# Order of additions, roundings, squares and weight splits at the seams of the second block

## The reference

```python
a = _rmsnorm(h, g_pre_mix[l])
u = jnp.einsum("bsd,dc->bsc", a, w_in[l])
# ... convolution, attention, w_out, h = h + _rmsnorm(y, g_post_mix[l])
f_in = _rmsnorm(h, g_pre_ffn[l])
gt = jnp.einsum("bsd,df->bsf", f_in, w_gate[l])
up = jnp.einsum("bsd,df->bsf", f_in, w_up[l])
```

## Time and profile before

| | |
|---|---|
| median of 3 runs | 1757.17 us (1757.05 to 1759.24) |
| profiled execution: its time | 1758.98 us |
| profiled execution: span from first to last instruction | 1757.2 us |
| mean granted TensorE clock | 0.995 |
| TensorE busy | 1716.0 us (98%) |
| VectorE busy | 1256.5 us (72%) |
| ScalarE busy | 818.7 us (47%) |
| transfers | 158.29 MB, mean 90 GB/s |

### The profile page before, as it was taken

The page is one execution under the profiler, slowest core; times in us unless marked ns, Lnnn a source line. Parts: engine busy times, 40 slices in busy tenths (PEclk is TensorE's granted clock), DMA queues, the critical chain, the costliest instruction groups (busy, mean ns, idle before and its releaser), DMA issues.

```text
span 1757.2 us, 21518 instructions
## 1 busy us (share of the span) xinstructions
PE 1716.0 (98%) x8215; PEld 1413.4 (80%) x8215; DVE 1256.5 (72%) x1915; ACT 818.7 (47%) x1345; POOL 37.8 (2%) x87
## 2 busy tenths in 40 slices
PE   8999999999999999999999999999999999999998
PEld 7887888888888777778888888788888788888886
DVE  6666358687888667765778788889987645765766
ACT  7433244343445656764433443542767532333342
POOL 0000000000001121000000000000000000000000
PEclk9999999999999999999999999999999999999999
DMA  7222442333412211116142423033100353234212
GB/s 251 84 73 84 129 135 76 117 97 107 136 45 62 64 49 61 48 49 192 48 144 71 134 72 120 12 98 106 49 13 13 90 174 96 72 92 141 66 49 84
DMA packets 195749, 158.29 MB, mean 90 GB/s; under 512 B 5248, under 2 KB 161280, under 8 KB 195648
## 3 DMA queue, kind: packets, MB, share of 16 engines
q1 hardware_dynamic: 194240, 154.16, 29.1%
q0 software_dynamic: 400, 1.25, 0.3%
q10 hardware_dynamic: 1008, 1.53, 0.2%
HBM read 154.81 MB, written 2.10 MB: 89 GB/s over the span
## 4 chain that ended last, share of the span: by engine, by line
PE 89%; DVE 6%; ACT 3%; issue 1%; DMA 0%; POOL 0%; DVEq 0%; SPq 0%; ACTq 0%
PE ps L1061 28%; PE ps L1063 28%; PE ps L1062 28%; PE ps L1565 1%; PE ps L1131 1%; ACT sb L2021 1%; DVE sb L2238 1%; ACT sb L1764 1%; PE ps L1454 0%; DVE sb L2236 0%; DVE sb L2495 0%; DVE sb L2264 0%; PE ps L1190 0%; DVE sb L2737 0%; ACT sb L1770 0%
## 5 line engine op out<-in xcount | busy, mean ns | idle before, releaser
L1061 PE MATMUL ps<-sb,sb 128*128 128x512 f32 (+3 forms) x2435 | 927.6, 387 | 9.7 <-ACT sb L2021 5.2
L1063 PE MATMUL ps<-sb,sb 128*128 128x512 f32 (+3 forms) x2435 | 911.6, 379 | 0.0
L1062 PE MATMUL ps<-sb,sb 128*128 128x512 f32 (+3 forms) x2435 | 910.9, 379 | 0.0
L2238 DVE TENSOR_TENSOR sb<-sb,sb 128x1024 fp32r<-128x1024 f32 (+1 forms) x414 | 404.8, 997 | 219.0 <-ACT sb L1764 218.2
L1061 PEld LDWEIGHTS ps<-sb,sb 128*128 128x128 f32 (+1 forms) x2435 | 450.8, 188 | 110.2 <-issue 11.9
L1764 ACT ACTIVATE sb<-sb 128x1024 fp32r<-128x1024 f32 (+1 forms) x414 | 349.7, 871 | 394.3 <-PE ps L1063 389.1
L1063 PEld LDWEIGHTS ps<-sb,sb 128*128 128x128 f32 (+1 forms) x2435 | 450.4, 188 | 86.6
L1062 PEld LDWEIGHTS ps<-sb,sb 128*128 128x128 f32 (+1 forms) x2435 | 451.1, 188 | 81.8 <-issue 0.2
L2478 DVE TENSOR_TENSOR sb<-sb,sb 128x1024 fp32r<-128x1024 f32 x70 | 85.5, 1222 | 47.5 <-ACT sb L1926 45.2
L1921 ACT ACTIVATE sb<-sb 128x512 f32<-128x512 f32 x64 | 40.3, 631 | 130.8 <-DVE sb L2530 130.8
L2460 DVE TENSOR_TENSOR sb<-sb,sb 128x1024 f32<-128x1024 f32 x80 | 95.1, 1217 | 0.6
(11 more groups left out here) (217 smaller groups left out, 1107.2 us busy)
## 6 DMA issues: line engine op xcount, KB each, us to landing
sb<-in_w_up SPq DMA_DIRECT2D x86, 512.0 KB, 4.1
sb<-in_w_down SPq DMA_DIRECT2D x86, 512.0 KB, 4.8
sb<-in_w_gate SPq DMA_DIRECT2D x22, 512.0 KB, 3.9
sb<-in_a_w_in SPq DMA_DIRECT2D x20, 512.0 KB, 3.8
sb<-in_w_in SPq DMA_DIRECT2D x20, 512.0 KB, 3.7
sb<-in_w_o SPq DMA_DIRECT2D x16, 512.0 KB, 3.7
sb<-in_w_mem_kv SPq DMA_DIRECT2D x8, 512.0 KB, 7.5
sb<-in_w_out SPq DMA_DIRECT2D x8, 512.0 KB, 3.8
```

What stands on the lines that cost most here:

```text
L1061: mm(ps, lh, rh, start=start, stop=False, **k)
L1062: mm(ps, lh, rl, start=False, stop=False, **k)
L1063: return mm(ps, ll, rh, start=False, stop=stop, **k)
L2238: tt(lo, raw, hi, ALU.subtract).then_inc(S("w_lo"), parts)
```

## The change

Two kinds of order are changed; no instruction is added or removed.

For the second layer of the first block (l = 1) alone, the last two additions of the feed-forward, `("rd", 3, 6)`, come ahead of the split of slab g0 (the `w` step). On ScalarE and TensorE this swap changes nothing, as only VectorE has a `rd` step.

At both seams ScalarE rounds columns 4 to 7 directly behind columns 0 to 3, then splits the second tile's slab, then squares row slabs 2 and 3; before, it was squares, split, columns 4 to 7. VectorE likewise forms the remainders of columns 4 to 7 ahead of the second tile's slab.

```diff
-        plan += [("P", 3, 6), ("rd", 3, 5), ("rdu", 3, 0), ("w", PS[l, 3, 6] + 3), ("rd", 3, 6)]
+        plan += [("P", 3, 6), ("rd", 3, 5), ("rdu", 3, 0)]
+        plan += [("w", PS[l, 3, 6] + 3), ("rd", 3, 6)] if l == 0 else [("rd", 3, 6), ("w", PS[l, 3, 6] + 3)]
         return plan
...
             square(X, "pre_mix", t)
         for k in range(4):
             turn("pre_mix", Ah, "pre_mix", k)
+        for k in range(4, 8):
+            turn("pre_mix", Ah, "pre_mix", k)
+        weights(SL["in", "g0"] + 2)
         for t in range(2, 4):
             square(X, "pre_mix", t)
-        weights(SL["in", "g0"] + 2)
-        for k in range(4, 8):
-            turn("pre_mix", Ah, "pre_mix", k)
         rsqrt("pre_mix", 4)
...
             square(X, "pre_ffn", t)
         for k in range(4):
             turn("pre_ffn", Ah, "pre_ffn", k)
+        for k in range(4, 8):
+            turn("pre_ffn", Ah, "pre_ffn", k)
+        weights(SL["gt", 0] + 2)
         for t in range(2, 4):
             square(X, "pre_ffn", t)
-        weights(SL["gt", 0] + 2)
-        for k in range(4, 8):
-            turn("pre_ffn", Ah, "pre_ffn", k)
         rsqrt("pre_ffn", 4)
...
         for k in range(4):
             turn("pre_mix", Ah, Al, "pre_mix", k)
-        weights(SL["in", "g0"] + 2)
         for k in range(4, 8):
             turn("pre_mix", Ah, Al, "pre_mix", k)
+        weights(SL["in", "g0"] + 2)
         stats("pre_mix")
...
         for k in range(4):
             turn("pre_ffn", Ah, Al, "pre_ffn", k)
-        weights(SL["gt", 0] + 2)
         for k in range(4, 8):
             turn("pre_ffn", Ah, Al, "pre_ffn", k)
+        weights(SL["gt", 0] + 2)
         stats("pre_ffn")
```

## The result

The changed kernel took 1762.21 us (median of 19 runs, 1759.15 to 1763.84), the kernel before 1759.12 us in as many runs beside it (1756.76 to 1761.62): ratio 1.0018, 95% interval 1.0012 to 1.0024, so 3.2 us slower (2.1 to 4.2). The profiled execution of the changed kernel spans 1759.5 us, 2.3 more than that of before.

A forecast was written before the change was run, and what follows sets the result against it. The prediction took one long stream of TensorE matmuls (89% of the chain) as the bound. Its terms, -0.44 + 2.09 and one clock fall of 1.5, gave +3.15 us on 1757.17: 1760.3 us, range 1757.2 to 1762.2.

The forecast's parts named there:

- The base: The whole kernel: the summed differences were put on 1757.17 us, the median of the runs, not the profiled 1758.98.
- rival C: Both seams: both new pauses lower TensorE's clock, +4.65 to 5.05 us, some 1762.0 us; chance 0.23.
- A: The forecast itself: one clock fall in the two new pauses, 1760.3 us, bounds 1758.7 to 1760.6; chance 0.40.
- The additions (part 1): First into second block: additions ahead of g0's split end a 0.77 us TensorE stall; ScalarE's first rounding 0.98 us earlier.
- The order in seam 1: First into second transformer block: with the additions' gain, the spread transposes come only 0.44 us earlier, not 0.98.
- The order in seam 2: Into the gated feed-forward: squares wait behind columns 4 to 7, spread 2.09 us later; other end 0.55 us.
- The pause: TensorE before the spread transposes: stands still 2.56 us in the first seam, 2.5 us in the second.
- The clock: Each new TensorE pause lowers the clock with chance one half; a fall costs 1.5 us, so one fall counted.
- B: Both seams: the new pauses are too short for any clock fall, +1.65 us, 1758.8 us; chance 0.25.
- D: Feed-forward seam: tile at full clock, so nothing lost overall, +0.1 us, 1757.3 us; chance 0.09.
- E: Both seams: the early addition carries through and squares are hidden, -1 to -4 us, about 1754; chance 0.03.
- The queues behind: SyncE's loads waiting on raw buffers freed up to 3.1 us later: costed at nothing, being needed four tiles on.

The follow-up runs named there:

- x1_swap: The kernel before with only the two additions moved ahead of g0's split: median 1757.82 us against 1759.08, ratio 0.9989.
- x2_seam1_order: The kernel before with only the new order of roundings, split and squares from first into second block: 1759.92 us against 1759.14, ratio 1.0006.
- x3_seam2_order: The kernel before with only the new order of roundings, split and squares into the gated feed-forward: 1763.37 us against 1759.08, ratio 1.0015.
- x5: The changed kernel with ten thrown-away matmuls more in each pause before the spread transposes: 1760.79 us against 1759.08 before, ratio 1.0006.
- x7: The changed kernel with the second tile's split moved behind squares 2 and 3 and the root, both seams: 1761.30 us against 1759.14 before, ratio 1.0015.
- x8: The changed kernel run once more, unaltered, beside the same runs of before as its version with filled pauses: 1761.92 us against 1759.30, ratio 1.0017.
- x9: The changed kernel with ten thrown-away matmuls in each pause before the spread, run once more: 1760.72 us against 1759.30 before, ratio 1.0009.
- x4_early_squares: The kernel before with additions ahead, squares where ScalarE would wait, the root's first step ahead of the second tile's split on VectorE: 1755.53 us against 1759.08, ratio 0.9976.
- x6: The early-squares kernel with 16 and 12 thrown-away matmuls more in the two pauses ahead of the feed-forward seam's first tile: 1753.27 us against 1759.14 before, ratio 0.9968.

## Why the prediction held and where it failed

**The differences.** The forecast was +3.15 us; the ratio gives +3.2 (2.1 to 4.2), the medians +3.09. It forecast the changed kernel as slower by less than 0.2%, and that is what came. That it agrees to 0.1 us is partly luck: the order's two terms were right to 0.13 us, but of the clock's term the runs show only that it is about 1 to 2 us.

**The base was the step that failed.** I put the sum on the median of three runs, 1757.17 us; over 19 runs that median is 1759.12, 1.95 us higher. So the time came out at 1762.21 instead of 1760.3, just beyond the range's end of 1762.2. The profiled execution, 1758.98 us, against which the sum was made, lay 1.81 us above the three runs' median, and the prediction put the differences on the lower of the two without a reason. It was in fact an ordinary run of the middle group. The third of the three runs, 1759.24, said so already. The range was made of the differences' bounds alone, with nothing for the base, although the prediction itself says that runs differ by 2. On 1759.12 the same sum gives 1762.3.

For the same reason the time, which lies by rival C's 1762.0, is not a sign of C: no profile of the changed kernel shows two falls behind the spreads. Two smaller slips: A's upper bound by its own terms is 1760.5 and not 1760.6, and the range reaches C's far end (1757.17 + 5.05 = 1762.2), which it says it leaves out. And 0.2% was taken for about what a measurement of this kernel can tell from no change; the interval of the result is 0.06% on either side.

**The additions (part 1)**: ScalarE's first rounding was expected at 1134.77 and TensorE's first matmul at 1135.60; they came at 1134.72 and 1135.55, in a trace that stands 0.04 us earlier at the seam's first transpose. The added wait was 0.31 us on VectorE and the split was done 0.22 us ahead of the rounding, hidden as said. x1_swap shows that the 0.98 us reach the second tile if nothing else is changed.

**The order in seam 1**: column 7 at 1140.37, measured 1140.33; the squares' end at 1144.38, measured 1144.33; the spread at 1145.69, measured 1145.66. That the gain shrinks from 0.98 to 0.44 is confirmed by x1_swap (-0.99) and x2_seam1_order (+0.55 by itself).

**The order in seam 2**: 2.09 us expected, 1.96 measured, 2.04 in x3_seam2_order. The small difference is the low stretch of the clock: it began at 1398.20 in both traces, but the tile 0.36 us later, so fewer of its matmuls lay in it. Choosing the end that the trace showed was right. The other end, 0.55 with the tile at full clock, was not seen: each of the six profiles with columns 4 to 7 first in seam 2 (the changed kernel, x3, x5, x7, x8, x9) had a low stretch in that tile.

**The pause** was 2.39 us by the profile, not 2.56 and 2.5, which I had counted from the pace of the matmuls and not from the modelled end of the last.

**The clock** was put at one fall of 1.5 us in two pauses. The fall in the changed kernel's profile cost 1.57 us; filling both pauses gives back 1.2 us beside the same runs of before, and 0.0012 of the ratio (2.1 us) where the runs of before were others. Both profiles of the changed kernel (its own and x8_after_again) are rival A, a fall in seam 1 and none behind the spread of seam 2; B and C, none or two, were not seen in them, but two profiles don't exclude them for other runs. D and E are out: the spread of seam 2 came 2 us later in every profile with the changed order (the changed kernel, x3, x5, x8, x9).

**The queues behind**, put at nothing, cost nothing that the traces show: the two stay 1.10 us apart from 1150 to 1249, and behind seam 2 the distance is 2.32 us at the spread and 2.37 at the last matmul.

**The strict queue of ScalarE** is shown by the rows above: 0.36, 0.44 and 0.44 us of waiting in front of squares whose data had been ready since 1134. The statement of the Trainium skill ("TensorE: Matmul & The Clock Gate", section "Architectural detail: the array is 16× 32×32, not 1× 128×128") that this engine is strictly first-in, first-out agrees with them. x4_early_squares puts the same instructions in another order, on VectorE too, and its spread in seam 1 comes 2.1 us earlier than the changed kernel's (10.49 against 12.55).

## What to carry to other kernels

Where two chains meet, giving one engine's early slots to the chain that is paced by a third engine delays the other chain by up to the sum of those waits (here 1.24 and 2.53 us of waits gave delays of 0.55 and 2.0, as the other chain had been held by VectorE's remainders until then); put work that is ready into the slots in which the engine would wait, and work that only the next step needs last. Look at the step ahead of the wait, not at its stalls alone: seam 2 had no stall to win. An absolute forecast also needs the scatter of the base: the median of three runs was 2 us off, more than the sum of the edit's two order terms (1.65).

## What was not expected of the hardware

The same pause can lower the clock or not. Before L1061 at 1249.21 TensorE stood 1.82 us, and the clock stayed at 1.00:

```profile
1250.00:1254.00 4.00, 4.00 (x19) 3.30 (x18) 3.96 (x7) 3.66 (x7) 0.00 (x0) 1.00 0.41 131
```

In the changed kernel the pause at the same instruction was as long, and the clock fell 1.1 us behind it (the window from 1251.40 above):

```profile
1250.30 0.50 PE L1062 MATMUL ps<-sb,sb 128*128 128x512 f32 x1 [1.81 <-DVE sb L2761]
...
1251.62 0.63 PE L1064 MATMUL ps<-sb,sb 128*128 128x512 f32 x1
1252.05 0.63 PE L1062 MATMUL ps<-sb,sb 128*128 128x512 f32 x1
```

All eleven profiles have this pause, 1.81 to 1.83 us long. In five (the changed kernel, x4, x6, x7, x8) a low stretch began 1.1 to 1.5 us behind its end, in the other six none. The place of the pause in the execution does not divide them: with its end at 1250.30 the clock fell, at 1250.40 (x1_swap) it did not.

Apart from the kernel's first and last microseconds, each low stretch in these traces is about 3.4 us or 6.8 us long and costs up to half of it. The three groups of run times of before, 2 us apart, are groups of the clock too. Each run has its mean granted clock on record: 22 runs at 0.994 took 1760.4 to 1761.8 us, 38 at 0.995 took 1758.5 to 1759.8, and 14 at 0.996 to 0.998 took 1756.7 to 1757.7. One stretch of 3.4 us at half clock takes 0.001 from the mean, so by the means neighbouring groups differ by one or two falls of about 1.6 us. That is an estimate, as a mean does not show its stretches.
